# One core of a diffusion step: the RWKV scan with K and B transposed in the chain of states, row-half decay products, an unrolled tile loop and filler matmuls

## The chip, the cores and the metric

One Trainium2 chip, of which the program uses one core. The metric is the device time of one execution in microseconds (us); lower is better. TensorE is called PE, with its weight loads as PEld; VectorE is DVE, ScalarE is ACT, GpSimd is POOL, SyncE is SP.

## What is computed

One trunk layer for 512 latent tokens (`x_sample`) and 128 context tokens (`x_prompt`) with shared weights, all f32. The mixer projects the modulated input and feeds a Fourier branch and a bidirectional RWKV-7 scan with 16 heads of 64; both are merged, projected and normalised, and a mixture of 16 experts follows. The change is in the scan alone:

```python
def wkv7_scan(r, w, k, v, kk, a, s0, reverse):
    def step(S, inp):
        r_t, w_t, k_t, v_t, kk_t, a_t = inp
        sa = jnp.einsum('bhij,bhj->bhi', S, -kk_t)
        S = (S * w_t[:, :, None, :] + sa[..., None] * (kk_t * a_t)[:, :, None, :]
             + v_t[..., None] * k_t[:, :, None, :])
        y = jnp.einsum('bhij,bhj->bhi', S, r_t)
        return S, y
...
    w_log = -jax.nn.softplus(-(w_decay0 + jnp.einsum('btdr,drc->btdc', jnp.tanh(w_dn), w_decay_up))) - 0.5
    decay = jnp.exp(-jnp.exp(w_log))
    a_rate = jax.nn.sigmoid(a0 + jnp.einsum('btdr,drc->btdc', a_dn, a_up))
```

There is one scan per direction with its own decay and rate (`d` = 2 directions, rank `r` = 64 each).

## The kernel before

Four phases run one after the other: `front_phase` (projections, to about 445 us), `scan_phase` (to about 1400 us), `merge_phase`, and `expert_phase` with `combine_phase`. Only `scan_phase` (from L434) is touched.

**Tiling.** The 1024 channels are eight tiles of 128 (two heads each); the 640 tokens are five chunks of 128 (four latent, one context, `CT`). A scan over a chunk is written as matrix products. For each chunk, direction and head (four problems a chunk), masked pair products of K and B with R and the normalised key are made, a triangular 128x128 matrix is inverted by doubling, and then a short serial chain carries the state from chunk to chunk.

**One tile** is `body` on each engine:
- *Pair products* (`pair_products`, L874 to L889), chunk by chunk. DVE masks them (L1161), ACT copies the parts of the triangular matrix (L767, L768), and the output of the tile before is normalised between them (`norm`).
- *Six rounds of the inverse* (`z_step`, L905 and L911; `t_step`, L926 to L936) on three groups of chunks `b` = 0, 1, 2 (two, two and one chunk). POOL masks the block of each level (`m_off`, L668), and at the start makes the diagonal (`tt_start`, L649, L651) and the first T (`t_start`, L656, L660). ACT evicts Z (L776), DVE adds to the diagonal and to T (L1204, L1207, L1210).
- *The chain of states* (`part`): for the context, then latent chunks 0 to 3, X = products with V and the state (L952, L955), U = inverse times X (L961), S = the state's increment (L967: four 64x64 quadrant results), each for both directions. ACT copies X and U (L758, L761), DVE updates and scales the states (L1178, L1180, L1165, L1166). `output` (L976, L977, L981) is put between the steps. ACT evicts the output (L795) and the final states (L798).

**Front work of the next tile.** In the rounds of tile i, slots (three a round, one per group) hold the jobs that prepare tile i + 1. PE's job writes the PSUM tile `F[3]` (two banks, 1024 columns), ACT or DVE reads it and counts `s_free` up, and the next job waits for that; so jobs go strictly one by one, in the same order on PE, ACT and DVE. The slots are: decay of direction 0, norm of the keys, decay of direction 1, rates of both directions, V's transposes, the initial states', K's and B's transposes for direction 0, two empty for PE, K and B for direction 1, and the bonus. A decay or rate job is two matmuls on 64 of the 128 rows, of 512 and 128 columns (L821); a transposing job is five 128x128 transposes (L837). DVE does in the same slots the prefix sums (`decays`, L1062), `keys` (L1074 to L1082) and `operands` (L1089 to L1094). In each slot DVE does the front work first, and then waits for the products of the group.

**The loop.** Tiles 0 and 7 are written out; tiles 1 to 6 are a hardware loop with two tiles a turn on every engine (`tiles`, `Fori`), on SP another one. Semaphore targets inside it are computed from the loop's register.

```python
                for rd in range(TOP):
                    z_step(i, NGR * rd)
                    z_step(i, NGR * rd + 1)
                    for b in range(NGR):
                        if b == 1:
                            z_step(i, NGR * rd + 2)
                        if not last and PER_ROUND * rd + b < NSLOT:
                            front(PER_ROUND * rd + b, i + 1, 1 - m)
                        t_step(i, NGR * rd + b)
```

## Time and profile before

| | |
|---|---|
| time, median of 3 runs | 2767.99 us (2761.09 to 2768.16) |
| profiled execution | 2766.63 us, span 2764.8 us |
| mean granted clock of PE over the span | 0.927 |
| busy: PE / DVE / ACT / POOL | 2482.6 / 1002.9 / 612.9 / 358.5 us |
| instructions | 59730 |

The span runs from the first to the last instruction in the profile; some 1.8 us of the time lie around it. The granted clock is the share of TensorE's 2.4 GHz that the chip's throttle let through: 1.00 is 2.4 GHz and 0.50 is 1.2 GHz. Matmul durations are from start to a modelled end and overlap when matmuls follow each other, so a stretch is best priced from the start of one group to the start of the next. An f32 matmul is two instructions, a transpose is one. "issue" is idle time in which the engine waited for nothing that the profile shows.

### The profile page before, as it was taken

How to read it: one execution, taken by the hardware profiler on the slowest of the kernel's cores; microseconds unless marked ns; L12 is line 12 of the kernel's file. 1: busy time of each engine (PE TensorE's matmuls, PEld its weight loads, DVE VectorE, ACT ScalarE, POOL GpSimd, SP SyncE). 2: the span in 40 equal slices, each digit the busy share in tenths (PEclk: the TensorE clock that was granted, in tenths of full speed). 3: DMA queues.
4: the chain of work that ended last, by engine and by line, in shares of the span. 5: the costliest groups of instructions: out<-in, count | busy, mean ns of one | idle time of the engine just before them, and what ended most of it. 6: DMA issues, size and time to landing. Idle time of an engine off the chain costs nothing. (4 is left out here: it accounts for less than half of the span.)

```text
span 2764.8 us, 59730 instructions
## 1 busy us (share of the span) xinstructions
PE 2482.6 (90%) x26260; PEld 1565.3 (57%) x26260; DVE 1002.9 (36%) x1737; ACT 612.9 (22%) x1147; POOL 358.5 (13%) x405
## 2 busy tenths in 40 slices
PE   5999996888988888888959958999999999999993
PEld 3999985677777777877835432333333333333331
DVE  2344211747556475574411451111111222122114
ACT  2122222434435344353210010111111111111111
POOL 0000000414314043141200330000000000000000
PEclk8999997889889898898879969999999999999997
DMA  8363321000000000000073039999999999999984
GB/s 329 116 228 98 125 90 55 20 18 11 18 24 6 26 12 18 24 5 9 7 287 103 38 113 420 400 392 398 385 396 387 400 389 402 395 394 387 397 315 157
DMA packets 180734, 538.77 MB, mean 195 GB/s; under 512 B 13254, under 2 KB 53926, under 8 KB 180216
## 3 DMA queue, kind: packets, MB, share of 16 engines
q1 hardware_dynamic: 177400, 524.39, 49.1%
q0 software_dynamic: 3072, 10.49, 1.7%
q8 instruction: 213, 3.49, 0.5%
q14 instruction: 49, 0.40, 0.1%
HBM read 504.15 MB, written 30.70 MB: 193 GB/s over the span
## 5 line engine op out<-in xcount | busy, mean ns | idle before, releaser
L1699 PE MATMUL ps_h_lat<-w_piece,xT 128*64 128x512 f32 x2048 | 455.6, 598 | 8.9 <-DVE hidden L1821 7.5
L1699 PEld LDWEIGHTS ps_h_lat<-w_piece,xT 128*64 128x64 f32 x2048 | 145.6, 138 | 312.3 <-issue 312.3
L1724 PE MATMUL ps_y_lat<-w_piece,hiddenT 128*64 128x512 f32 x1024 | 232.6, 596 | 0.9 <-ACT hiddenT L1585 0.9
L1708 PE MATMUL ps_h_ctx<-w_piece,xT 128*16 128x512 f32 x2048 | 226.1, 593 | 0.0
L1815 DVE TENSOR_TENSOR hidden<-sigmoid_lat,ps_h_lat 64x1024 f32<-64x1024 f32 x32 | 39.1, 1223 | 506.8 <-ACT sigmoid_ctx L1591 506.8
L325 PE MATMUL ps_in<-hT_hi,w_in_hi 128*128 128x320 f32 x752 | 173.6, 312 | 3.0 <-issue 3.0
L668 POOL TENSOR_TENSOR Mo<-x,levels_sb 128x256 f32<-128x256 f32 x200 | 156.2, 803 | 129.8 <-PE ps_scan L905 129.8
L325 PE MATMUL ps_in<-hT_lo,w_in_hi 128*128 128x320 f32 x752 | 171.9, 310 | 0.0
L325 PE MATMUL ps_in<-hT_hi,w_in_lo 128*128 128x320 f32 x752 | 171.8, 310 | 0.0
L1724 PEld LDWEIGHTS ps_y_lat<-w_piece,hiddenT 128*64 128x64 f32 x1024 | 70.2, 137 | 138.3 <-issue 137.7
L930 PE MATMUL ps_scan<-Z,T 64*64 64x64 f32 x3200 | 127.0, 230 | 20.5 <-POOL T L660 12.7
L1708 PEld LDWEIGHTS ps_h_ctx<-w_piece,xT 128*16 128x16 f32 x2048 | 59.1, 97 | 139.7 <-issue 137.5
L905 PE MATMUL ps_scan<-TT_diag,Mo 64*64 64x64 f32 x3200 | 113.1, 222 | 27.8 <-issue 18.3
L1589 ACT ACTIVATE sigmoid_lat<-ps_h_lat 64x1024 f32<-64x1024 f32 x32 | 32.6, 1018 | 469.2 <-PE ps_h_lat L1699 469.2
L930 PEld LDWEIGHTS ps_scan<-Z,T 64*64 64x64 f32 x3200 | 111.6, 143 | 34.1 <-issue 29.9
L325 PEld LDWEIGHTS ps_in<-hT_hi,w_in_hi 128*128 128x128 f32 x752 | 126.1, 189 | 5.3 <-issue 5.1
L325 PEld LDWEIGHTS ps_in<-hT_lo,w_in_hi 128*128 128x128 f32 x752 | 126.4, 189 | 0.0
L325 PEld LDWEIGHTS ps_in<-hT_hi,w_in_lo 128*128 128x128 f32 x752 | 126.3, 189 | 0.0
L936 PE MATMUL ps_scan<-T,Z 64*64 64x64 f32 x3200 | 125.4, 230 | 0.0
L905 PEld LDWEIGHTS ps_scan<-TT_diag,Mo 64*64 64x64 f32 x3200 | 105.4, 139 | 30.4 <-issue 30.3
L1640 POOL DMA_INDIRECT x_scratch<-ye,row_out x16 | 22.8, 1428 | 737.5 <-DVE ye L1828 737.5
L1733 PE MATMUL ps_y_ctx<-w_piece,hiddenT 128*16 128x256 f32 x2048 | 116.7, 380 | 0.0
(276 smaller groups left out, 3605.6 us busy)
## 6 DMA issues: line engine op xcount, KB each, us to landing
w_piece<-in_w_e SPq DMA_DIRECT2D x192, 2048.0 KB, 14.0
w_ada<-in_w_ada SPq DMA_DIRECT2D x6, 4096.0 KB, 18.0
w_in_raw<-in_w_in SPq DMA_DIRECT2D x23, 1024.0 KB, 6.3
rkv_scratch<-projected SPq DMA_DIRECT2D x24, 320.0 KB, 6.4
rkv_T<-rkv_scratch SPq DMA_DIRECT2D x8, 960.0 KB, 5.1
gates_scratch<-projected SPq DMA_DIRECT2D x16, 320.0 KB, 6.8
gate_sb<-gates_scratch SPq DMA_DIRECT2D x8, 640.0 KB, 6.2
x<-in_x_sample SPq DMA_DIRECT2D x8, 512.0 KB, 5.7
```

The costliest lines, as they stand in the source:

```text
L325: last = pe.matmul(wide[c % 2][:, b * 512:b * 512 + HALF], w, h[:, k, b * HALF:(b + 1) * HALF], start=(k == 0 and n == 0), stop=(k == KD - ...
L668: ins = g_.tensor_tensor(Mo[:, p, :, :].rearrange("p (e h) n -> p e h n", e=2), Mq[:, ORDER[p], 0:2, :, :], levels[:, l, :, :].unsqueeze(2 ...
L905: last = pe.matmul(ps_of(b_z(b), b)[hs, c, q, :], Mo[hs, p, q, :], TD[hs, p, q, :], start=True, stop=True)
L930: last = pe.matmul(ps_of(b_z(b), b)[hs, c, q, :], T[hs, p, q, :], Z[hs, p, q, :], start=True, stop=True)
L936: last = pe.matmul(ps_of(b_dt(b), b)[hs, c, q, :], Z[hs, p, q, :], T[hs, p, q, :], start=True, stop=True)
L1589: act.activation(sg[UP, :], psA[UP, :], ACT.Sigmoid)
L1640: g_.indirect_dma_start(out=d["x1"], out_offset=bass.IndirectOffsetOnAxis(ap=row[j][:, 0:1], axis=0), in_=ye[j][:, :], in_offset=None, com ...
L1699: last = pe.matmul(psA[rows, cs], x[:, k, A], w[:, q, cs], start=(k == 0), stop=(k == KD - 1))
L1708: last = pe.matmul(psB[GRP[g], :], x[:, k, B], w[:, q, c * 512:(c + 1) * 512], start=(k == 0), stop=(k == KD - 1))
L1724: last = pe.matmul(psY[rows, :], hT[:, f, A], w[:, q, c * 512:(c + 1) * 512], start=(hf == 0 and f == 0), stop=(hf == 1 and f == FK - 1))
L1733: last = pe.matmul(psYB[GRP[g], 0:256], hT[:, f, B], w[:, q, g * 256:(g + 1) * 256], start=(hf == 0 and f == 0), stop=(hf == 1 and f == FK ...
L1815: v.tensor_tensor(hid[A, :], sg[UP, :], psA[UP, :], ALU.mult)
```

## The change

1. The loops are written out: all eight tiles on all engines, and SP's loop.
2. A decay or rate job does both directions at once. Direction 0 is on rows 0 to 63 and writes bank 0 of `F[3]`, direction 1 is on rows 64 to 127 and writes bank 1. The first job of each kind does 512 columns, the second 128. ACT evicts each with two activations. DVE's `decays` wait for both decay jobs, its `keys` for both rate jobs.
3. The transposes of K and B leave the slots. K of direction 0 is turned in the last round, B of direction 0 and K and B of direction 1 in the chain, between U and S of steps 0, 1 and 2. Before the first tile they stand behind the bonus.
4. S is two full 128x128 products for each direction instead of quadrant products (the parts across heads are not read).
5. `fill(n)`: n matmuls of 384 bf16 columns whose result nobody reads, into columns 640 to 1023 of `F[0]`, in the last round and in the chain. In the last tile they take the place of the transposes in the chain.
6. POOL starts T (`t_start`) directly behind each group's first mask instead of behind the masks of all groups.

```diff
-    (J_DEC0, J_NORM, J_DEC1, J_RATE0, J_RATE1, J_VT, J_ST, J_KT0, J_BT0, J_NONE0, J_NONE1, J_KT1, J_BT1, J_BONUS) = range(14)
+    (J_DEC0, J_DEC1, J_NORM, J_RATE0, J_RATE1, J_VT, J_ST, J_SCAN1, J_SUB1, J_KEYS1, J_NONE0, J_NONE1, J_NONE2, J_BONUS) = range(14)
+    TURNS = (J_KT0, J_BT0, J_KT1, J_BT1) = range(NSLOT, NSLOT + 4)
+    TURN_AT = {0: J_BT0, 1: J_KT1, 2: J_BT1}
@@ tiles (every engine; SP's loop in the same way)
-            body(0, 0, True, False)
-            with eng.Fori(0, (KD - 2) // 2) as j:
-                body(2 * j + 1, 1, False, False)
-                body(2 * j + 2, 0, False, False)
-            body(KD - 1, 1, False, True)
+            for i in range(KD):
+                body(i, i % 2, i == 0, i == KD - 1)
@@ POOL, body
                     m_off(b)
-                for b in range(NGR):
                     t_start(b)
@@ ACT, front
-                    act.activation(dst[:, :], ps, ACT.Sigmoid, bias=c[:, col:col + 1]).then_inc(s_free, 1)
+                    for dr in range(2):
+                        ins = act.activation(dst[dr][:, c0:c1], F[3][:, dr * 512:dr * 512 + c1 - c0], ACT.Sigmoid, bias=c[:, col + dr:col + dr + 1])
+                    ins.then_inc(s_free, 1)
-                for at, dr, which in ((J_RATE1, 0, (0, 1)), (J_VT, 0, (2,)), (J_BT0, 1, (0, 1)), (J_NONE1, 1, (2,))):
+                for at, dr, which in ((J_VT, 0, (0, 1)), (J_ST, 0, (2,)), (J_KEYS1, 1, (0, 1)), (J_NONE1, 1, (2,))):
@@ ACT, body
+                if not last:
+                    front(J_KT0, i + 1, 1 - m)
                 for n in CHAIN:
                     part(i, n, "X")
                     part(i, n, "U")
+                    if not last and n in TURN_AT:
+                        front(TURN_AT[n], i + 1, 1 - m)
@@ PE, front
-                    for c0, c1 in wide:
-                        last = pe.matmul(F[3][:, c0:c1], w[a:a + LORA, :], x[a:a + LORA, c0:c1], start=True, stop=True)
+                    for dr, rows in enumerate(HALVES):
+                        last = pe.matmul(F[3][:, dr * 512:dr * 512 + c1 - c0], w[rows, :], x[rows, c0:c1], start=True, stop=True)
@@ PE
+            def fill(n):
+                for _ in range(n):
+                    pe.matmul(F[0][:, TOK:1024], causal[:, 0, 0, :], causal[:, 0, :, :], start=True, stop=True)
+            def turn(n, i, m, last):
+                if not last:
+                    front(n, i + 1, 1 - m)
+                elif n != J_KT0:
+                    fill(3)
@@ PE, part, "S"
-                        for w, x in ((Bt[m][dr], U(dr, c)), (Kt[m][dr], Vt[m][:, c, :])):
-                            for hs in HALVES:
-                                last = pe.matmul(Sps[hs, hs], w[:, c, hs], x[:, hs], start=(w is Bt[m][dr]), stop=(w is Kt[m][dr]))
-                        last.then_inc(s_sn, 1)
+                        pe.matmul(Sps, Bt[m][dr][:, c, :], U(dr, c), start=True, stop=False)
+                        pe.matmul(Sps, Kt[m][dr][:, c, :], Vt[m][:, c, :], start=False, stop=True).then_inc(s_sn, 1)
@@ PE, body
                     z_step(i, NGR * rd + 1)
+                    if rd == TOP - 1:
+                        turn(J_KT0, i, m, last)
...
+                        if rd == TOP - 1 and b:
+                            fill(2)
                         t_step(i, NGR * rd + b)
+                fill(3)
                 pe.wait_ge(s_full, i * NGR + NGR)
                 part(i, m, CT, "X")
                 part(i, m, 0, "X")
+                fill(2)
                 part(i, m, CT, "U")
                 part(i, m, 0, "U")
+                turn(TURN_AT[0], i, m, last)
                 part(i, m, CT, "S")
                 part(i, m, 0, "S")
                 output(m, CT)
+                fill(1)
+                for n in (1, 2):
+                    part(i, m, n, "X")
+                    fill(2)
+                    part(i, m, n, "U")
+                    turn(TURN_AT[n], i, m, last)
+                    part(i, m, n, "S")
+                    if n == 1:
+                        fill(3)
                 output(m, 1)
+                fill(2)
                 part(i, m, 3, "X")
@@ DVE, front: the same work in other slots
+                if n == J_DEC1:
                     decays(i, 0, 0)
                 if n == J_NORM:
                     decays(i, 0, 1)
-                if n == J_DEC1:
+                if n == J_RATE0:
...
-                if n == J_RATE0:
+                if n == J_RATE1:
                     keys(i, m, 0)
-                if n == J_RATE1:
+                if n == J_VT:
                     operands(i, m, 0, (0, 1))
-                if n == J_VT:
+                if n == J_ST:
                     operands(i, m, 0, (2,))
-                if n == J_ST:
+                if n == J_SCAN1:
                     decays(i, 1, 0)
-                if n == J_KT0:
+                if n == J_SUB1:
                     decays(i, 1, 1)
-                if n == J_BT0:
+                if n == J_KEYS1:
                     keys(i, m, 1)
```

## Rows read from the trace of the kernel before

**Rows 1.** The page, busy tenths in 40 slices: TensorE's granted clock.

```profile
PEclk8999997889889898898879969999999999999997
```

**Rows 2.** The tile of the output, its eviction; duration min/median/max, first and last start.

```profile
L795 ACT ACTIVATE y_T<-ps_scan x8: 703/703/704, 608.3 to 1386.1; 128x640 f32<-128x640 f32 x8
```

**Rows 3.** Windows: length, busy us (instructions) by engine, granted clock, DMA share, GB/s.

```profile
857.12:872.15 15.03, 12.90 (x252) 10.84 (x254) 12.28 (x18) 9.40 (x11) 13.00 (x17) 0.89 0.01 2
893.03:905.93 12.90, 9.67 (x251) 9.10 (x249) 12.60 (x18) 4.24 (x9) 4.70 (x5) 0.87 0.01 3
905.93:914.90 8.97, 8.97 (x245) 8.07 (x243) 5.34 (x9) 2.28 (x4) 0.00 (x0) 1.00 0.01 4
919.84:952.38 32.54, 30.08 (x258) 27.20 (x258) 7.43 (x28) 5.55 (x21) 0.00 (x0) 0.74 0.11 34
1310.38:1355.46 45.08, 39.94 (x1280) 39.37 (x1280) 23.64 (x40) 10.98 (x24) 21.89 (x32) 0.96 0.03 11
```

**Rows 4.** Timeline, a middle tile's first round: start, duration, engine, operation, [idle before, releaser].

```profile
861.20 1.26 POOL L660 TENSOR_TENSOR T<-T,eye_sb 128x512 f32<-128x512 f32 x1
862.61 1.98 PE L930 MATMUL ps_scan<-Z,T 64*64 64x64 f32 x32 [2.13 <-POOL T L660]
867.89 1.15 PE L930 MATMUL ps_scan<-Z,T 64*64 64x64 f32 x32
869.90 1.34 PE L821 MATMUL ps_scan<-lora,w_dec 64*128 64x512 f32 x4
871.17 0.68 PE L930 MATMUL ps_scan<-Z,T 64*64 64x64 f32 x16
```

**Rows 5.** Timeline, PE, the last pair products of the same tile.

```profile
853.50 0.71 PE L874 MATMUL ps_scan<-AR,K 64*128 64x256 f32 x4
855.11 0.39 PE L883 MATMUL ps_scan<-B,AR 64*64 64x64 f32 x10
```

**Rows 6.** Timeline, DVE and PE, rounds one to four of the same tile.

```profile
862.73 4.40 DVE L1062 TENSOR_TENSOR_SCAN G_T<-one_sb,sg 128x128 f32<-128x128 f32 x5 [2.26 <-ACTq L698]
887.62 2.25 DVE L1062 TENSOR_TENSOR_SCAN G_T<-one_sb,sg 128x128 f32<-128x128 f32 x5
904.25 0.77 PE L837 MATMUL ps_scan<-ident_sb,K 128*128 128x128 f32 x5 [1.06 <-DVEq L1097]
906.63 0.41 DVE L1210 TENSOR_TENSOR T<-T,ps_scan 128x256 f32<-128x256 f32 x1
```

**Rows 7.** Timeline, PE: a front-phase product, and the chain at full clock.

```profile
439.81 0.46 PE L325 MATMUL ps_in<-hT_hi,w_in_lo 128*128 128x320 f32 x2
934.50 0.34 PE L967 MATMUL ps_scan<-x,Bt 128*64 128x64 f32 x4
944.63 0.44 PE L955 MATMUL ps_scan<-x,AR 128*128 128x128 f32 x2
944.90 0.56 PE L952 MATMUL ps_scan<-Vt,NRR 128*128 128x64 f32 x4
```

**Rows 8.** Timeline and windows: first pair products behind a jump, and without one.

```profile
838.36 0.95 PE L874 MATMUL ps_scan<-AR,K 64*128 64x256 f32 x4 [2.04 <-issue]
953.38 0.71 PE L874 MATMUL ps_scan<-AR,K 64*128 64x256 f32 x4 [1.00 <-ACT state_out L798]
838.36:842.62 4.26, 4.08 (x57) 3.53 (x57) 2.04 (x4) 0.00 (x0) 0.00 (x0) 0.60 0.12 21
953.38:955.77 2.39, 2.39 (x57) 2.20 (x57) 1.47 (x4) 0.00 (x0) 0.00 (x0) 1.00 0.08 14
```

**Rows 9.** Timeline, PE, before the first tile: B1's transposes, then the bonus.

```profile
494.15 1.33 PE L837 MATMUL ps_scan<-ident_sb,B 128*128 128x128 f32 x5 [0.79 <-ACT Kt L717]
496.27 2.50 PE L841 MATMUL ps_scan<-bonus,headones_sb 128*128 128x512 f32 x4 [0.79 <-ACT Bt L717]
```

**Rows 10.** Windows in the front phase, around 20 transposes of x.

```profile
50.40:53.50 3.10, 3.02 (x12) 1.85 (x10) 3.10 (x6) 2.51 (x6) 0.00 (x0) 0.50 1.02 410
53.50:56.00 2.50, 0.00 (x0) 0.00 (x0) 2.50 (x5) 2.42 (x6) 0.00 (x0) 0.97 1.02 410
```

More of the change, by code:

```diff
@@ L457, in scan_phase @@
     PER_ROUND = 3
-    (J_DEC0, J_NORM, J_DEC1, J_RATE0, J_RATE1, J_VT, J_ST, J_KT0, J_BT0, J_NONE0, J_NONE1, J_KT1, J_BT1, J_BONUS) = range(14)
+    (J_DEC0, J_DEC1, J_NORM, J_RATE0, J_RATE1, J_VT, J_ST, J_SCAN1, J_SUB1, J_KEYS1, J_NONE0, J_NONE1, J_NONE2, J_BONUS) = range(14)
     NSLOT = J_BONUS + 1
+    TURNS = (J_KT0, J_BT0, J_KT1, J_BT1) = range(NSLOT, NSLOT + 4)
     N_BONUS, N_GATE = 5, 6
-    JOBS = [n for n in range(NSLOT) if n not in (J_NONE0, J_NONE1)]
+    JOBS = [n for n in range(NSLOT + 4) if n not in (J_SCAN1, J_SUB1, J_KEYS1, J_NONE0, J_NONE1, J_NONE2)]
     NJ = len(JOBS)
@@ L610, in _ @@
             load_rkv(2)
-            with sp.Fori(1, KD - 2) as i:
+            for i in range(1, KD - 2):
                 store_states(i - 1)
@@ L691, in front @@
                 if n in (J_DEC0, J_DEC1, J_RATE0, J_RATE1):
-                    dst, col = {J_DEC0: (sg[0], C_DEC0), J_DEC1: (sg[1], C_DEC0 + 1), J_RATE0: (rate[0], C_RATE0),
-                                J_RATE1: (rate[1], C_RATE0 + 1)}[n]
+                    dst, col = (sg, C_DEC0) if n in (J_DEC0, J_DEC1) else (rate, C_RATE0)
+                    c0, c1 = wide[n in (J_DEC1, J_RATE1)]
                     done(n)
@@ L798, in body @@
                 act.activation(state_out[:, :, :], bank(5)[:, 0:2 * P].rearrange("p (e n) -> p e n", e=2), ACT.Copy).then_inc(s_sos, 1)
-            for n in range(NSLOT):
+            for n in range(NSLOT + len(TURNS)):
                 front(n, 0, 0)
@@ L817, in front @@
                     w, x = (w_dec, lora[0]) if n in (J_DEC0, J_DEC1) else (w_rate, lora[1])
-                    a = LORA * (n in (J_DEC1, J_RATE1))
+                    c0, c1 = wide[n in (J_DEC1, J_RATE1)]
                     pe.wait_ge(s_wup, 32 * i + 32)
-                    for c0, c1 in wide:
-                        last = pe.matmul(F[3][:, c0:c1], w[a:a + LORA, :], x[a:a + LORA, c0:c1], start=True, stop=True)
+                    for dr, rows in enumerate(HALVES):
+                        last = pe.matmul(F[3][:, dr * 512:dr * 512 + c1 - c0], w[rows, :], x[rows, c0:c1], start=True, stop=True)
                 if n == J_NORM:
@@ L1012, in body @@
                 output(m, CT)
-                part(i, m, 1, "X")
-                part(i, m, 1, "U")
-                part(i, m, 1, "S")
-                part(i, m, 2, "X")
-                part(i, m, 2, "U")
-                part(i, m, 2, "S")
+                fill(1)
[7 more added lines that the diff above has]
+                        fill(3)
                 output(m, 1)
+                fill(2)
                 part(i, m, 3, "X")
@@ L1031, in _ @@
             pe.wait_ge(s_masks, 1)
-            for n in range(NSLOT):
+            for n in range(NSLOT + len(TURNS)):
                 front(n, 0, 0)
@@ L1057, in decays @@
                 if half_ == 0:
-                    v.wait_ge(s_sig, 4 * i + (1, 2)[dr])
+                    v.wait_ge(s_sig, 4 * i + 2)
                     if dr == 1:
@@ L1071, in keys @@
             def keys(i, m, dr):
-                v.wait_ge(s_sig, 4 * i + 3 + dr)
+                v.wait_ge(s_sig, 4 * i + 4)
                 v.tensor_scalar(B[dr][:, :], rate[dr][:, :], -1.0, cur[m][:, C_KA:C_KA + 1], ALU.add, ALU.mult)
@@ L1130, in front @@
                 if n == J_BONUS:
-                    v.wait_ge(s_job, NJ * i + NJ)
+                    v.wait_ge(s_job, NJ * i + JOBS.index(J_BONUS) + 1)
                     v.tensor_tensor(bonus[m][:, :], ps[:, 0:TOK], v_, ALU.mult).then_inc(s_free, 1)
```

## The prediction

> **What bounds the kernel now.** The page comes first. The granted clock of TensorE (PEclk) is 9 or 10 tenths nearly everywhere, but reads 7 to 9 through slices 8 to 20, where the scan runs [rows 1]. The scan works through eight channel tiles in a row, and each evicts its output once. From the first eviction to the last there are (1386.1 - 608.3) / 7 = 111 us a tile [rows 2]. The change touches nothing outside this phase.
>
> Next the windows, cut at the borders of one middle tile and of the last one [rows 3]. Three things are to be seen. In the first round of triangular inverses (857.12 to 872.15) PE is busy for 12.9 of 15.0 us; in the fourth (893.03 to 905.93) for 9.7 of 12.9, while DVE is busy for 12.6. The last tile has no front work of a next tile, and does all six rounds in 45.1 us, against 919.84 - 857.12 = 62.7. And the chain of states (919.84 to 952.38) takes 32.5 us, of which PE is busy for 30.1, at a mean granted clock of 0.74. With two levels, 0.5 and 1.0, that is (1 - 0.74) x 2 x 32.5 = 16.9 us at 1.2 GHz. So TensorE is the bound of the chain, half of it at half clock, and DVE is the bound in the middle of the rounds.
>
> **The change part by part**, for a middle tile, first the rounds.
>
> *Start of T (POOL).* The first product with T waits 2.13 us for POOL, and then runs at half clock: 1.98 us for 32 matmul instructions, against 1.15 a little later [rows 4]; with the equal stretch behind it that is 2 x 0.83 = 1.7. The start of T now comes behind each group's first mask, some 7 us earlier for group 0. POOL then reaches the mask of group 2 later by two starts of T, of which the addition alone is 1.26 us [rows 4]; a PE job and the first T product stand before its user, so that costs nothing. Without that cover, in the last tile, I charge 1.5 us.
>
> *Decay and rate products.* One job of 640 columns takes 871.17 - 869.90 = 1.27 us [rows 4], so four are 5.1. On row halves the nearest row is the pair products, whose row halves also alternate: 4 x 384 columns in 855.11 - 853.50 = 1.61 us, 1.05 ns a column against 2.0 [rows 5]. The two directions together are 1280 columns: 1.34 us if they overlap as well as that, 2.54 if not at all. A single pair of long products overlaps only in its middle, so I take 1.75, which saves 0.8 for each kind, 1.6 a tile. ACT pays for it: four evictions become eight shorter ones. DVE's scan now waits for both decay jobs, so it starts about 2.3 us later than at 862.73 [rows 6]; but DVE has by then done the first two additions of the round.
>
> *K and B leave the rounds.* A transposing job is 0.77 us of PE, and that of K1 also waits 1.06 us for DVE's drain [rows 6]. Three leave the rounds outright; K0's stays in the last round, where PE waits for evictions anyway.
>
> *What DVE makes of it.* PE alone would gain 2.1 + 1.7 + 1.6 + 3 x 0.77 + 1.06 = 8.8 us. But DVE works almost without a pause from the scan at 862.73 to the last addition of round four at 906.63 + 0.41 [rows 6], and its work is only put in another order. I followed it slot by slot with the old durations: scan at 865.0, one scan at 4.40 us and one at 2.25 (the slow one runs beside POOL), and the last diagonal addition of round four at about 905.2. PE then has left one product of the third group (0.6, from its half size), the bonus job (1.3, like a decay job), the T products of the second group (869.90 - 867.89 = 2.0 [rows 4]) and of the third (1.1): 5.0 us, so it ends at 910.2, against 914.90 now [rows 3]. That is 4.7 us. PE now has gaps of some 2 us in rounds four and five where it waits for DVE; a fall of the clock there takes back up to 1.5. I take **4.0** a tile, with 1 and 8 as ends.
>
> **The chain.** Scaled to full clock, today's is 32.5 - 16.9 / 2 = 24.1 us. Added are:
> - S as full products: four instructions of 0.135 (two of this shape take 944.90 - 944.63 = 0.27) in place of eight that take about 0.32 (four of them are in sight for 0.34, tail included, and both halves overlap), so +0.22, eight times: 1.8 us [rows 7].
> - Three transposing jobs: 3 x 0.77 = 2.3 us.
> - 15 idle-filling products of 384 bf16 columns. No row shows one. The nearest is the one-instruction product of 320 columns in the front phase, two of which end within 0.46 us, at most 0.23 each and less where they overlap [rows 7]; the other bound is f32 at the decay job's 2.0 ns a column, 0.77. I take 0.18, near the first: 2.7 us. Seven more stand in the last round, in time in which PE waits.
>
> The sum is 30.9. About 1 us of the added work falls into waits that are in today's 32.5, but the step over DVE (state, scaled state, next X) keeps its length: I take **30.5**, a gain of 2.0. ACT's copies of K and B go behind the copies of U, while PE does S and output. The full gain hangs on the clock: h us at half clock cost h / 2.
>
> **The unrolled loop.** At its jump back PE stands for 2.04 us instead of 1.00, and the first pair products then run at half clock, 4.26 us instead of 2.39 [rows 8]. That is 2.9 us, at two places (the loop runs three times): 5.6 with rounding.
>
> **Prologue.** Tile 0's transposes of K0 and B0 lay beside DVE's work; now all four stand behind the bonus job and ahead of the first pair products. A job and its eviction are 496.27 - 494.15 = 2.12 us at half clock [rows 9]. Two more on the path are 4.2; the shorter row-half jobs give back about 1. I charge 3.
>
> **Sum.** Seven tiles with front work: 7 x (4.0 + 2.0) = 42. Jumps 5.6. Last tile: no decay job stands before its first T product, so the wait is 2.1 + 1.3, and 1.7 of half clock; less the 1.5 charged that is 3.6; its chain (fills in place of transposes) I leave as it is. Prologue -3. In all 48.2 us. The profiled execution took 2766.6 us (span 2764.8 and 1.8 around it), so **2718 us**. It lies 1.4 us below the median of the runs, 2767.99, which changes nothing.
>
> **The rivals.**
>
> *The clock stays up and DVE is not the bound (faster).* Rounds gain 6 to 7 rather than 4, because POOL's earlier end also frees DVE, and chains come to 29. That gives 48.2 + 7 x (2.5 + 1.5) = 76, 2690 us. For it: the last tile's rounds are 17.6 us shorter, so much of a middle tile's round is not its own work. Against: DVE's 12.6 of 12.9 us. Chance 0.2.
>
> *The clock falls once in each chain.* One stretch like today's second (8 us) costs 4 us a chain, 32 in all: 2750 us. For it: today the clock falls in waits and in the small X and U products, and these remain. Against: every such place now has a fill or wide columns beside it. Chance 0.2.
>
> *Half clock as often as today (slower).* If the added products don't keep the clock up, the chain has its 16.9 us at half clock and all the added work: 30.5 + 8.5 = 39.0, 6.5 longer than now, or 52 for eight chains. The gains outside the chains are 28 + 5.6 + 3.6 - 3 = 34, so the kernel ends 18 us slower: 2785 us. It decides from 4.2 us a chain, that is from some 12.5 us at half clock. For it: the chain is at half clock already with PE busy for nine tenths of it. Against it is the front phase: transposes alone, 12 of them between 50.40 and 53.50 at granted 0.50, and the clock then stands at 0.97 without anything else having run on PE [rows 10]. Chance 0.08. The Trainium skill ("TensorE: Matmul & The Clock Gate", Part 4: PE-mode transpose) states that transpose mode does not count as PE activity in the way that matmuls do. By that, the transposes in the chain would weaken it, and this rival would be the result; the row of the front phase speaks the other way.
>
> *The change doesn't do what it says:* the row halves run one behind the other (2.54 us for each kind). Then PE gains nothing there, but DVE's wait for both decays grows by 0.8: 7 x 0.8 = 6 us less gain, 2724. That lies inside the forecast.
>
> **How the numbers follow.** The forecast, 2718, has 0.5, with an own range of 2703 to 2737 (rounds' gain 2 to 6 us). The rivals have 0.2 (2690), 0.2 (2750), 0.08 (2785); 0.02 is left for the unforeseen. The range reaches to the inner parts of both large rivals: 2684 to 2752. Faster by over 0.3% (8.3 us, about what a measurement of this kernel can tell from no change) are all but the slower rival and the upper end of the clock rival: 0.87. Within 0.3%: 0.06, slower: 0.07.
>
> **What would show it.** Right: a period of 105 to 107 us from one eviction of the output to the next; windows over the chain at clock above 0.9 and 30 to 31 us long; no wait on POOL's T; pair products in 2.39 us at every tile's start; five transposes in the shadow of the U copies; PE waiting on DVE's additions in rounds four and five. Wrong: a chain of over 34 us, or a clock near 0.74 in it; DVE waiting longer for the sigmoids in round one than rounds four and five give back; fills of over 0.3 us each.

## The result, and the profile after

| | before | after |
|---|---|---|
| time, median of 4 runs | 2765.05 us (2761.09 to 2768.16) | 2687.45 us (2682.59 to 2688.05) |
| profiled execution | 2766.63 us, span 2764.8 | 2687.13 us, span 2685.2 |
| mean granted clock over the span | 0.927 | 0.961 |
| busy: PE / DVE / ACT / POOL | 2482.6 / 1002.9 / 612.9 / 358.5 us | 2420.9 / 984.9 / 615.4 / 363.8 us |

The medians are 77.6 us apart; the ratio estimated from all runs is 0.9706 [0.9686, 0.9727]. The direction was right. The time lies inside the outer range of 2684 to 2752 us, near its lower end, and outside the forecast's own 2703 to 2737; the gain is 1.6 times the 48 us worked out.

The page of the kernel after, its line of the granted clock and that of the output's eviction (the tile's view):

```profile
PEclk8999998799999999999889969999999999999997
```

```profile
L798 ACT ACTIVATE y_T<-ps_scan x8: 703/703/703, 601.4 to 1307.2; 128x640 f32<-128x640 f32 x8
```

The dip through the scan [rows 1] is gone: slices 9 to 19 (537 to 1275 us) all have a 9, the highest digit. From the first eviction to the last there are (1307.2 - 601.4) / 7 = 100.8 us a tile against 111 [rows 2].

Windows over tile 2 of the kernel after: its six rounds one by one, all six, the chain, and the first pair products of the tile; columns as in [rows 3]:

```profile
721.44:733.04 11.60, 10.53 (x253) 8.68 (x254) 8.40 (x14) 7.44 (x12) 10.12 (x15) 1.00 0.01 3
733.04:743.16 10.12, 9.91 (x260) 8.55 (x257) 9.61 (x15) 7.39 (x12) 5.09 (x5) 1.00 0.01 3
743.16:751.63 8.47, 7.74 (x248) 7.38 (x246) 7.80 (x13) 4.99 (x11) 4.81 (x5) 1.00 0.02 5
751.63:761.05 9.42, 7.84 (x248) 7.38 (x243) 9.05 (x17) 3.02 (x7) 4.37 (x5) 1.00 0.02 3
761.05:771.40 10.35, 8.60 (x228) 7.63 (x230) 10.01 (x16) 2.20 (x4) 0.00 (x0) 1.00 0.01 3
771.40:777.15 5.75, 5.61 (x116) 3.98 (x111) 2.93 (x6) 3.13 (x10) 0.00 (x0) 1.00 0.29 88
...
721.44:777.15 55.71, 50.24 (x1324) 43.60 (x1324) 47.79 (x76) 28.17 (x54) 24.40 (x30) 1.00 0.04 12
777.15:805.98 28.83, 27.28 (x253) 24.28 (x253) 7.42 (x28) 8.22 (x25) 0.00 (x0) 1.00 0.12 36
...
704.73:707.12 2.39, 2.39 (x57) 2.20 (x57) 1.46 (x4) 0.00 (x0) 0.00 (x0) 1.00 0.10 18
```

Against [rows 3]: the first round lost 15.03 - 11.60 = 3.4 us, the fourth 12.90 - 9.42 = 3.5. The fifth is longer, 10.35 against 8.97, and DVE is busy for 10.01 of it: the wait for DVE has moved there. The chain fell from 32.5 to 28.8 us, though three transposing jobs and 12 fills were added in it (three more fills stand ahead of it), and its clock is 1.00.

The same windows over all eight tiles, in us:

| stage | before | after | difference | foreseen |
|---|---|---|---|---|
| rounds, tiles 0 to 6 | 444.0 | 391.4 | -52.6 | -28 |
| rounds, last tile | 45.1 | 45.0 | 0 | -3.6 |
| eight chains | 252.3 | 230.4 | -21.9 | -14 |
| pair products and gaps ahead of them | 145.1 | 139.2 | -5.9 | -5.6 |
| start of the first pair products | 499.7 | 501.2 | +1.5 | +3 |

The mean of tiles 1 to 6 (called the middle tiles from here) is 63.4 us of rounds before and 55.9 after, and 31.9 and 28.8 of chain. So the miss is the rounds, and less of it the chains. The clock has a part in the rounds too: in the middle tiles it is 0.92 to 0.97 before and 1.00 after.

### The profile page after: what moved, and what is told of

Read it like the earlier page. It is cut to its first block and busy times, and to the rows that moved or that the text cites. A ratio compares the mean times of both kernels' runs of the same rounds, so it can differ in the third digit from the quotient of the medians.

```text
span 2685.2 us, 58051 instructions
## 1 busy us (share of the span) xinstructions
PE 2420.9 (90%) x26165; PEld 1504.4 (56%) x26165; DVE 984.9 (37%) x1737; ACT 615.4 (23%) x1179; POOL 363.8 (14%) x405
## 5 line engine op out<-in xcount | busy, mean ns | idle before, releaser
L666 POOL TENSOR_TENSOR Mo<-x,levels_sb 128x256 f32<-128x256 f32 x200 | 161.9, 832 | 99.2 <-PE ps_scan L908 99.1
L933 PE MATMUL ps_scan<-Z,T 64*64 64x64 f32 x3200 | 119.2, 221 | 5.9 <-ACT Z L775 5.3
L933 PEld LDWEIGHTS ps_scan<-Z,T 64*64 64x64 f32 x3200 | 106.1, 136 | 22.8 <-issue 19.5
L1186 DVE TENSOR_TENSOR NRR<-ps_scan,causal_sb 128x384 f32<-128x384 f32 x160 | 78.0, 548 | 106.2 <-PE ps_scan L878 106.0
L939 PE MATMUL ps_scan<-T,Z 64*64 64x64 f32 x3200 | 116.5, 219 | 0.4 <-issue 0.4
```

Source lines behind the costliest of these rows:

```text
L666: ins = g_.tensor_tensor(Mo[:, p, :, :].rearrange("p (e h) n -> p e h n", e=2), Mq[:, ORDER[p], 0:2, :, :], levels[:, l, :, :].unsqueeze(2 ...
L933: last = pe.matmul(ps_of(b_z(b), b)[hs, c, q, :], T[hs, p, q, :], Z[hs, p, q, :], start=True, stop=True)
L939: last = pe.matmul(ps_of(b_dt(b), b)[hs, c, q, :], Z[hs, p, q, :], T[hs, p, q, :], start=True, stop=True)
L1186: v.tensor_tensor(NRR[:, p, :, :], src[:, 0:3 * P].rearrange("p (a n) -> p a n", a=3), causal[:, dr, :, :], ALU.mult).then_inc(s_am, 1)
```

## The experiments

The measured values in one table; rounds and chain are means of the middle tiles. Before, after, the run without fills, before with fills, POOL's order and both prologue runs are medians of four runs; the others ran once. The kernel before alone ranged from 2757.7 to 2775.4 us over all its runs, so a single time says little, and the windows carry the argument.

| run | time | middle rounds | middle chain, clock |
|---|---|---|---|
| before | 2765.05 | 63.4 | 31.9, 0.74 to 0.78 |
| after | 2687.45 | 55.9 | 28.8, 1.00 |
| after, no fills | 2693.08 | 55.6 | 30.1, 0.84 to 1.00 |
| after, T late | 2701.96 | 58.2 | 28.8, 1.00 |
| before, with fills | 2742.71 | 63.4 | 28.5, 1.00 |
| after, transposes in slots, no fills | 2720.32 | 58.7 | 29.5, 0.79 to 1.00 |
| after, transposes in slots | 2704.51 | 58.8 | 28.6, 1.00 |
| after, one direction a job | 2700.47 | 57.0 | 28.8, 1.00 |
| after, POOL's order | 2687.48 | 55.8 | 28.8, 1.00 |
| after, loops | 2695.97 | 55.9 | 29.1, 1.00 |
| after, prologue | 2683.10 | 56.0 | 28.8, 1.00 |
| after, prologue, fewer fills | 2683.02 | 56.3 | 28.5, 1.00 |
| before, T early | 2757.20 | 61.1 | 31.6, 0.74 to 0.78 |
| before, unrolled | 2755.21 | 63.4 | 31.0, 0.73 to 0.83 |

Theory A is the prediction's: DVE bounds the middle of the rounds and hides most of what PE saves. Theory B is the rival that DVE is not the bound and the clock stays up.

### Without fills

```diff
-                for _ in range(n):
+                for _ in range(0):
```

> The changed kernel without its filler products (the transposes and the full products of S stay in the chain). Theory A, the fillers hold the clock: the chain's granted clock falls from 1.00 to under 0.9 and the chain (28.8 us) gets longer, 29 to 32 us, although it has 15 products of 0.16 us less; the kernel is 5 to 30 us slower than the changed one. Theory B, the wide products of S and the transposes hold it alone: clock 1.00, chain 26.5 to 27.5 us, the kernel 10 to 20 us faster than the changed one.

2693.08 us, ratio to before 0.9737 [0.9720, 0.9754]. Windows over the chains of tiles 1, 2 and 3:

```profile
674.85:702.75 27.90, 25.85 (x241) 23.16 (x241) 7.43 (x28) 8.24 (x25) 0.00 (x0) 1.00 0.12 38
...
775.70:808.13 32.43, 30.38 (x241) 27.66 (x241) 7.42 (x28) 8.25 (x25) 0.00 (x0) 0.84 0.10 33
...
881.56:912.40 30.84, 28.79 (x241) 26.04 (x241) 7.42 (x28) 8.25 (x25) 0.00 (x0) 0.89 0.11 35
```

The same 241 instructions take 27.90 us where the clock stays at 1.00 (three of the eight chains) and up to 32.43 where it falls. So the fills (12 of the 15; three stand ahead of the first X) cost 28.83 - 27.90 = 0.93 us a chain and 0.3 in the rounds, and save up to 4.5 where the clock would have fallen. Where it falls, the timeline of the second of these chains shows:

```profile
775.70 1.55 PE L967 MATMUL ps_scan<-Vt,NRR 128*128 128x64 f32 x12 [0.65 <-ACT x L787]
...
778.34 1.81 PE L976 MATMUL ps_scan<-Xs,x 128*128 128x64 f32 x8
780.68 1.97 PE L976 MATMUL ps_scan<-Xs,x 128*128 128x64 f32 x8 [0.53 <-ACT Xs L757]
```

U is 1.81 us at half clock against 1.00 at full, behind the waits for ACT at the chain's start. The fills are worth 2693.08 - 2687.45 = 5.6 us net here. Without them the loss is small because the work that the change brings into the chain already holds the clock in part: over tiles 0 to 6 the chains' mean clock is 0.93 here, against 0.75 in the kernel before.

### Start of T late again

```diff
                     m_off(b)
+                for b in range(NGR):
                     t_start(b)
```

> The changed kernel with T started behind the masks of all groups again. Theory C, POOL's place decides about DVE: the wait for T returns (about 2.1 us), the clock falls in round one, DVE's scans lengthen again (2.8 and 1.7 us to above 3.5 and 2.2), and the rounds of a middle tile go from 55.8 to 60 us or more. Theory D, only the wait itself: rounds 57 to 58 us, DVE's durations unchanged. The last tile's rounds (45.0) change by less than 1 us under both.

2701.96 us. The middle rounds grow by 2.3 us and DVE's busy time in them is the same, 47.7 against 47.8. PE in the first round of tile 2 of this kernel:

```profile
729.71 1.57 PE L934 MATMUL ps_scan<-Z,T 64*64 64x64 f32 x26 [2.45 <-issue]
```

The wait is back, at the place of [rows 4], with some half clock behind it. The DVE timeline shows how it reaches the end: every addition to the diagonal, from the first to the fifteenth, starts 2.4 to 3.3 us later after the start of the rounds than in the changed kernel. DVE's scan waits for the sigmoids, they wait for the decay jobs, and those for the T product. So DVE's chain of work does not hide a wait in round one; it is moved by it as a whole. Theory A had a DVE that goes on while PE waits. Part of the 2.3 us is clock: the two middle tiles at 1.00 take 57.5 us, 1.8 more than the changed kernel's 55.7, and the four at 0.94 or 0.97 take 58.4 to 58.7.

### The kernel before with fills

```diff
+            def fill(n):
+                for _ in range(n):
+                    pe.matmul(F[0][:, TOK:1024], causal[:, 0, 0, :], causal[:, 0, :, :], start=True, stop=True)
@@ body: in the last round and the chain, at the places of the change, three for each turn in the chain
```

> The kernel before with filler products at the places of the changed kernel (three more where that one has transposes). Theory A, the clock is the matter of the chain: granted clock near 1.00 in the chains, 27 to 29 us each instead of 30.3 to 32.7; rounds unchanged; 25 to 40 us faster than before. Rival: the clock still falls in the narrow X and U products, chain 33 to 36 us, 10 to 30 us slower than before.

2742.71 us, ratio 0.9916 [0.9897, 0.9936]. A window over the chain of tile 3 of this kernel:

```profile
911.00:939.63 28.63, 25.89 (x279) 21.69 (x279) 7.42 (x28) 5.56 (x21) 0.00 (x0) 1.00 0.13 38
```

Against the 32.54 us of [rows 3], 21 more instructions and 3.9 us less. The eight chains lose 252.3 - 227.2 = 25.1 us, which is the whole gain, and the rounds stay at 63.4. Fills alone give more in the chains than the change does (21.9), since S and the transposes aren't lengthened or added. They give a little under a third of its gain of 79.6 us in the span.

### Transposes back in the slots, without and with fills

```diff
-    (..., J_ST, J_SCAN1, J_SUB1, J_KEYS1, J_NONE0, J_NONE1, J_NONE2, J_BONUS) = range(14)
+    (..., J_ST, J_KT0, J_BT0, J_KEYS1, J_NONE0, J_NONE1, J_KT1, J_BT1, J_BONUS) = range(15)
-    TURN_AT = {0: J_BT0, 1: J_KT1, 2: J_BT1}
+    TURN_AT = {}
```

> The changed kernel without fillers and with the transposes of K and B back in slots of the rounds, one by one. If transposes count as activity for the clock, the chain has a lower granted clock here than in the run without fillers; if they do not count (the rule of the Trainium skill), it is equal or higher. With the clock as in the kernel before (0.74 to 0.78) the chain is 30 to 32 us, at full clock about 25. Rounds get longer by the four jobs: 57 to 60 us instead of 55.8.

> The changed kernel with the transposes of K and B back in slots of the rounds (three fillers stand in their places in the chain). From the pair of runs without fillers (58.7 against 55.6 us) the rounds of a middle tile are about 3.2 us longer than the changed kernel's 55.9, so 59; the chain is 28.4 us as in the kernel before with fillers, clock 1.00. If instead the moved jobs only filled PE's waits, the rounds stay under 57.

2720.32 us without fills and 2704.51 us with. Against their counterparts with the transposes in the chain the middle rounds grow by 3.2 and 2.9 us. At full clock the chain is 26.53 us without transposes and without fills (two of eight chains), against 27.90 with: 0.46 us for each transposing job. With fills in the transposes' place it is 28.62 against 28.83. So four jobs moved out of the slots save 2.9 us and cost 0.2 as long as something has to hold the clock anyway. Of the 2.9 us about 1 is clock: the rounds with fills and transposes in slots take 57.6 us where they are at 1.00 and up to 60.5 at 0.94.

The two runs without fills bear on the clock. Windows over the chains of tiles 1, 2 and 5, transposes in slots, no fills:

```profile
683.46:710.00 26.54, 24.62 (x226) 21.81 (x226) 7.43 (x28) 5.45 (x21) 0.00 (x0) 1.00 0.15 46
...
785.12:815.74 30.62, 28.98 (x226) 26.30 (x226) 7.43 (x28) 5.46 (x21) 0.00 (x0) 0.83 0.13 40
...
1102.93:1135.00 32.07, 30.43 (x226) 27.70 (x226) 7.43 (x28) 5.45 (x21) 0.00 (x0) 0.79 0.12 38
```

Over tiles 0 to 6 the mean clock of the chains is 0.87 here, and 0.93 with the three transposing jobs between U and S (the last tile has none in either kernel). The transposes did not weaken the clock; that they helped it is not shown by seven chains of each, of which two and three stood at 1.00. The Trainium skill ("TensorE: Matmul & The Clock Gate", Part 4: PE-mode transpose) states that a transpose does not count as PE activity in the way a matmul does, and by that the chains with transposes would stand lower. With [rows 10] this is the second place of this case that does not agree with it.

### One direction for each decay and rate job

```diff
-                    for dr, rows in enumerate(HALVES):
-                        last = pe.matmul(F[3][:, dr * 512:dr * 512 + c1 - c0], w[rows, :], x[rows, c0:c1], start=True, stop=True)
+                    a = LORA * (n in (J_DEC1, J_RATE1))
+                    for c0, c1 in wide:
+                        last = pe.matmul(F[3][:, c0:c1], w[a:a + LORA, :], x[a:a + LORA, c0:c1], start=True, stop=True)
```

> The changed kernel with one direction for each decay or rate job, 640 columns on 64 rows, in the new order of slots. If row halves save PE time on the path: rounds of a middle tile 1.0 to 2.5 us longer than 55.9. If DVE sets the rounds: under 0.5 us longer, since DVE waits for both jobs in any case and PE has gaps of 4 us in rounds three to five. The jobs themselves go from 1.05 + 0.42 to 1.27 + 1.27 us.

2700.47 us; the middle rounds grow by 1.1 us (56.7 to 57.0 us in the four tiles at 1.00, against 55.7 to 56.4). Tile 0's rounds grow by 5.5, at a clock of 0.92 against 1.00, and the first pair products start 2.2 us later. In the changed kernel PE's timeline has the two jobs of a kind:

```profile
723.46 1.13 PE L824 MATMUL ps_scan<-lora,w_dec 64*128 64x512 f32 x4
724.51 1.15 PE L933 MATMUL ps_scan<-Z,T 64*64 64x64 f32 x32
...
727.27 0.68 PE L908 MATMUL ps_scan<-TT_diag,Mo 64*64 64x64 f32 x16 [0.67 <-POOL Mo L666]
728.35 0.49 PE L824 MATMUL ps_scan<-lora,w_dec 64*128 64x128 f32 x4 [0.40 <-ACT sg L695]
728.77 0.33 PE L933 MATMUL ps_scan<-Z,T 64*64 64x64 f32 x4
```

Start to start they take 724.51 - 723.46 = 1.05 and 728.77 - 728.35 = 0.42 us, 1.47 a kind for 1280 columns: 1.15 ns a column. The row halves do overlap, nearly as well as the pair products.

### POOL's order

In the last tile PE waits at a new place, 6 us after the start of the rounds (timeline of the changed kernel):

```profile
1239.81 0.68 PE L908 MATMUL ps_scan<-TT_diag,Mo 64*64 64x64 f32 x15 [2.08 <-POOL Mo L666]
...
1240.39 1.81 PE L933 MATMUL ps_scan<-Z,T 64*64 64x64 f32 x30
```

That is group 2's mask, which POOL now makes behind two starts of T, and half clock behind the wait. The run puts the starts of groups 1 and 2 behind it:

```diff
                 for b in range(NGR):
                     m_off(b)
-                    t_start(b)
+                    if b == 0:
+                        t_start(0)
+                t_start(1)
+                t_start(2)
```

> The changed kernel with T of groups 1 and 2 started behind the mask of group 2. In the changed kernel the third product waits 0.67 us for that mask in middle tiles and 2.08 us in the last tile, where the clock then falls. Expected: those waits gone, rounds of a middle tile 0.5 to 1.1 us shorter, the last tile's 2 to 4 us; 6 to 10 us faster than the changed kernel. Against it: T of group 1 comes later than its user, and a wait of the same size appears at the T product of group 1: under 2 us.

2687.48 us, ratio 0.9710 [0.9683, 0.9737]: no difference. In the middle tiles the wait of 0.67 us for the mask is gone, but the second decay job then waits 0.74 for ACT instead of 0.40. In the last tile a wait of 1.31 us for T and one of 0.54 for the masks of round two replace the one of 2.08. POOL is simply behind PE there, in either order.

### The loops back

```diff
-            for i in range(KD):
-                body(i, i % 2, i == 0, i == KD - 1)
+            body(0, 0, True, False)
+            with eng.Fori(0, (KD - 2) // 2) as j:
+                body(2 * j + 1, 1, False, False)
+                body(2 * j + 2, 0, False, False)
+            body(KD - 1, 1, False, True)
```

> The changed kernel with the hardware loops put back. At the two jumps back PE stands for about 1 us more and the first pair products run at half clock (1.9 us): 5 to 6 us slower, in the pair stages of tiles 3 and 5 alone. If the chain's full clock carries over the jump, only the stand remains: 2 us.

2695.97 us; the last tile ends 8.1 us later. PE behind the second jump back (timeline):

```profile
1019.29 0.71 PE L880 MATMUL ps_scan<-AR,K 64*128 64x256 f32 x4 [2.43 <-issue]
1020.04 0.90 PE L880 MATMUL ps_scan<-AR,K 64*128 64x256 f32 x4
```

The stand is like that of [rows 8], and the pair products behind it run partly at half clock: the stage takes 18.8 us, against 16.7. Behind the first jump the stage takes 18.1 us at a clock of 1.00, so there it is not the clock; PE stands once more in it, for 0.72 us. The two jumps cost 6.1 us in all (2.6 in the gaps, 3.5 in the stages). The looped tiles without one also lose 0.3 us in the pair products, and all six 0.3 in the chain, where no jump is near. That makes 9.0 us; the start, tile 0 and the last tile's rounds (43.2 us against 45.0, the same instructions) differ besides.

### The kernel before with T early, and the kernel before unrolled

```diff
                     m_off(b)
-                for b in range(NGR):
                     t_start(b)
```

> The kernel before with the start of T put directly behind each group's first mask and nothing else changed. Undoing this part in the changed kernel cost 2.3 us a tile in the rounds. If the parts of the rounds' gain add up, the six middle tiles' rounds fall here from 63.4 to about 61.1 us and the span by 16 us, to 2749. If DVE takes it back in the middle of the rounds (the theory of the prediction: PE alone gains more than the rounds do), they fall by less than 1 us and the span by less than 8.

2757.20 us, span 2755.4. The middle rounds fall to 61.1 us: 2.3, as much as the undoing cost in the changed kernel. So this part is worth the same in both kernels. Here too some of it is clock (0.97 to 1.00 in the middle rounds, 0.92 to 0.97 before). The last tile ends 1385.9 - 1371.4 = 14.5 us earlier, near the 16 expected. The span falls only by 9.4: the other 5 us are lost behind the scan, in phases that the edit doesn't touch.

> The kernel before with its loops of tiles written out and nothing else changed. Putting the loops back into the changed kernel cost 8.5 us: about 5 at the jumps and 0.3 us for each chain and pair stage of a looped tile. I expect 8 us less here, a span of 2757, with the pair stages of tiles 3 and 5 at 17 us and the two long gaps ahead of them gone. If instructions that take their semaphore targets from a register also cost time in the rounds, these become shorter than 63.4 by up to 1.2 us, which is what the other parts leave unexplained of the rounds' gain, and the span falls by 15.

2755.21 us, span 2753.4. The edit is that of the loops, the other way round. The pair stages are 16.7 us in tiles 1 to 7, the long gaps are gone, and the rounds are 63.4 us as before: unrolling is no part of their gain. From the first pair products to the last tile's end it is 886.2 - 875.8 = 10.4 us less, of which 3.6 are the chains (248.7 against 252.3): up to 1.7 by the 0.3 us of each looped chain, the rest the clock's chance.

### Prologue, and fewer fills

The timeline of the changed kernel ahead of its first tile has four jobs in a row, each 2.1 us at half clock:

```profile
493.60 1.33 PE L840 MATMUL ps_scan<-ident_sb,K 128*128 128x128 f32 x5 [0.92 <-DVE bonus L1157]
495.73 1.33 PE L840 MATMUL ps_scan<-ident_sb,B 128*128 128x128 f32 x5 [0.79 <-ACT Kt L716]
497.85 1.33 PE L840 MATMUL ps_scan<-ident_sb,K 128*128 128x128 f32 x5 [0.79 <-ACT Bt L716]
499.97 1.33 PE L840 MATMUL ps_scan<-ident_sb,B 128*128 128x128 f32 x5 [0.79 <-ACT Kt L716]
501.23 1.23 PE L877 MATMUL ps_scan<-AR,K 64*128 64x256 f32 x4
```

```diff
+    FIRST = list(range(J_ST + 1)) + [J_KT0, J_BT0] + list(range(J_ST + 1, J_BONUS)) + [J_KT1, J_BT1, J_BONUS]
-            for n in range(NSLOT + len(TURNS)):
+            for n in FIRST:
```

> The changed kernel with one other order of the jobs of tile 0, before the first tile: the transposes of K0 and B0 follow those of the initial states, those of K1 and B1 stand ahead of the bonus job instead of behind it. Tiles 1 to 7 are as they were. The run with all transposes in the slots reached its first pair products at 496.9 us against 501.2, so I expect the first pair products at 497 to 498 and the time 3.5 to 4.5 us under that of the changed kernel: 2683 us. The rival: the prologue is bound by DVE and the pair products start at most 1 us earlier, 2687 us.

2683.10 us (2681.99 to 2684.76), ratio 0.9705 [0.9674, 0.9736]. The first pair products start at 497.2, 4.0 us earlier, but the last tile ends only 2.5 us earlier: the clock is 0.94 and 0.97 in the rounds of tiles 0 and 1, where it was 1.00. That is not shown to come of the new order: with the old one the clock in tile 0's rounds is also 0.94 in the runs with POOL's order and with loops, and their first pair products start at 502.1 and 501.7. The medians are 4.3 us apart, but the spreads of the two kernels overlap, and the estimated ratios to the kernel before are 0.9705 and 0.9706. That this version is faster as a whole is not shown.

```diff
                 output(m, CT)
-                fill(1)
...
                 output(m, 1)
-                fill(2)
```

> As the run before it, and three of the fifteen idle-filling products of a chain are left out: the one behind the output of the context and the two behind the output of chunk 1, where outputs of full width have just run. If those outputs hold the granted clock by themselves, the chain loses about 3 x 0.16 us less whatever lay in waits: 28.4 to 28.6 us against 28.8, clock 1.00 in all eight, and the time is 2 to 3 us under that of the run before. If the fills hold the clock there, some chains fall to 0.8 to 0.9 as without any fill and are 30 to 32 us long, and the time is 5 us or more over that of the run before.

2683.02 us, ratio 0.9704 [0.9672, 0.9735]. The chains are 28.50 us and at 1.00, so these three fills held nothing in them. But the 2.6 us won are not in the time: tiles 3 and 5 now also have a fall of the clock in their rounds (0.97), each some 0.7 us, and 1.6 us more lie behind the scan, which the edit doesn't touch.

## Why the prediction was right or wrong

**Start of T (right in kind, and DVE did not hide it).** The wait of 2.13 us and the half clock behind it are gone: the first T product follows the decay job without idle time. PE's own saving was worked out as 3.8; 2.3 arrived in the rounds, in both kernels alike. A new wait of 0.67 us for the mask of group 2, priced at nothing, stands in the first round; where the rest went is not shown.

**Decay and rate products (right).** 1.47 us a kind against 1.75 foreseen, and 1.1 us of rounds against the 1.6 of PE alone. That the row halves run one behind the other did not happen.

**K and B leave the rounds (right).** 2.9 us of rounds, about 1 of it clock, of the 3.4 that PE alone was given for them.

**"What DVE makes of it" (the step that failed).** It took 4.0 us of PE's 8.8; measured are 63.4 - 55.9 = 7.5. Three undone parts give 2.3 + 2.9 + 1.1 = 6.3, almost 2 of it by clock; the other 1.2 were not isolated (the order of the jobs and the pairing of evictions went with them). The term that was mis-sized is the time at which DVE reaches the last addition to the diagonal in round four. Followed slot by slot with old durations it came 48.1 us after the start of the rounds. In tile 2 it comes 45.2 after:

```profile
730.09 2.81 DVE L1086 TENSOR_TENSOR_SCAN G_T<-one_sb,sg 128x128 f32<-128x128 f32 x5 [2.75 <-ACTq L697]
...
751.01 1.68 DVE L1086 TENSOR_TENSOR_SCAN G_T<-one_sb,sg 128x128 f32<-128x128 f32 x5
...
766.63 0.41 DVE L1229 TENSOR_TENSOR TT_diag<-TT_diag,ps_scan 128x256 f32<-128x256 f32 x1
```

The last row is that addition: 766.63 - 721.44 = 45.2. The first scan starts 8.65 us after the start of the rounds, where 7.9 were foreseen, but the two take 4.49 us together and not 6.65 as in [rows 6]. DVE's busy time in the middle rounds fell from 50.3 to 47.8 us for the same instructions. With the later start of the scan, the last addition comes 48.1 - 45.2 = 2.9 us before the time worked out. The 0.7 charged for falls of the clock in PE's new gaps did not come, the clock is 1.00. And the base was low: tile 3 has 62.7 us of rounds, the mean 63.4, which holds more falls of the clock. These are 4.3 us for the missing 3.5; 0.8 is taken back in round six, which with K0's transposes and the fills is 5.75 us against 4.94. DVE was indeed nearly without a pause there, and PE does wait 1.04 and 1.52 us in the first products of rounds four and five (timeline of PE), each until 0.10 us after one of DVE's additions has ended:

```profile
753.80 1.15 PE L908 MATMUL ps_scan<-TT_diag,Mo 64*64 64x64 f32 x32 [1.04 <-issue]
...
763.71 0.41 PE L908 MATMUL ps_scan<-TT_diag,Mo 64*64 64x64 f32 x6 [1.52 <-issue]
```

So the bound was named rightly and its length taken as fixed, which it was not. What sets the length of the scans is POOL's work beside them. POOL's timeline around the first scan of the tile, before (the scan runs from 862.73 to 867.13) and after (from 730.09 to 732.90):

```profile
862.42 1.41 POOL L656 TENSOR_TENSOR T<-x,levels_sb 128x256 f32<-128x256 f32 x2
863.97 1.27 POOL L660 TENSOR_TENSOR T<-T,eye_sb 128x512 f32<-128x512 f32 x1
866.81 3.88 POOL L668 TENSOR_TENSOR Mo<-x,levels_sb 128x256 f32<-128x256 f32 x5
...
728.57 3.41 POOL L666 TENSOR_TENSOR Mo<-x,levels_sb 128x256 f32<-128x256 f32 x5
734.23 4.30 POOL L666 TENSOR_TENSOR Mo<-x,levels_sb 128x256 f32<-128x256 f32 x4 [2.24 <-PE ps_scan L908]
```

Before, POOL is busy during all five scans, the one beside its addition of 512 columns taking 1.48 us. After, it is done at 731.98: three scans take 0.70 to 0.82 us, the two behind them 0.39 each. It is so in the traces of all 14 kernels: a group of five with no POOL instruction beside it takes 1.68 or 1.69 us, whatever ACT does, and the others take 2.10 to 4.44. The edits that move POOL's instructions and nothing else move the first scan: 4.40 to 3.78 us with T early in the kernel before, 2.81 to 2.97 or 3.62 with T late and to 3.16 with POOL's other order in the changed one. Other work of DVE from SBUF behaves alike (the product `rate`, 0.82 alone and 1.29 beside POOL); the additions that read PSUM do not (0.68 either way). The prediction had noted that the slow scan runs beside POOL, moved POOL's starts of T ahead of it, and kept 4.40 and 2.25 us.

**The chain (clock right, size too small).** 28.8 us against 30.5. S costs 0.11 us an instruction rather than 0.135, as the timeline has it:

```profile
782.29 0.72 PE L840 MATMUL ps_scan<-ident_sb,B 128*128 128x128 f32 x5
782.84 0.39 PE L980 MATMUL ps_scan<-x,Bt 128*128 128x128 f32 x2
783.06 0.39 PE L981 MATMUL ps_scan<-Vt,Kt 128*128 128x128 f32 x2
783.29 0.39 PE L980 MATMUL ps_scan<-x,Bt 128*128 128x128 f32 x2
```

A direction is 783.29 - 782.84 = 0.45 us, and a transposing job 0.55 rather than 0.77. On the path the three jobs cost 1.4 us (2.3 foreseen) and the fills 0.9 (2.7). The rest of the sum was 24.1 + 1.8 = 25.9 and measured 26.5, without jobs and fills at full clock. The price of a fill itself was near, two take 0.33 us, 0.16 each against 0.18; but three of the 15 stand ahead of the chain (they were counted among the seven of the last round as well), and of the other twelve (1.9 us) half lie in waits. The last tile's chain, which I left as it was, gained too: its fills hold the clock, 28.6 against 30.8.

**The unrolled loop (right, too small).** 5.6 foreseen (its own terms, 2.9 twice, give 5.8); the two jumps cost 6.1, and the 0.3 us a stage that looped tiles lose besides, 2.9 in all, were not foreseen. On the last tile's end it was 8.1 us.

**The last tile (wrong).** Foreseen was a gain of 3.6 with 1.5 charged for POOL. POOL's mask of group 2 is 2.08 us late and has half clock behind it, as the T had, and POOL's other order gives 45.0 us too. The size is not sharp: the same instructions take 43.2 to 45.4 us in the six kernels that have them, T early alone brought 45.1 to 43.9 in the kernel before, and without the seven fills it is 43.7. So a part of the gain is there, and the fills may take it back.

**Prologue (right).** Four transposing jobs at 2.1 us stand behind the bonus. The +1.5 of the table is one pair of executions: with this prologue the first pair products start at 501.2 to 502.7 us in five kernels, with that of before at 496.9 to 500.7 in four, 2.9 on average, and 3 were foreseen. What the shorter jobs give back is lost in that spread.

**The rivals.** What came is the first one, "the clock stays up and DVE is not the bound", in its time (2690 foreseen) and its rounds (6 to 7 us) and chains (29), though its reason is only half right: DVE still bounds the middle, with shorter instructions. Its own "for", the last tile's rounds, was no evidence. That the clock falls once a chain is what happens without fills. Half clock in the chains as often as today did not come in any run that has fills.

## What to carry to other kernels

- A wait in the first stage of a pipelined stretch passes to its end even if a second engine is busy throughout the middle, when that engine's work starts behind the wait. Ask what its first instruction waits for before hiding a saving behind its busy share.
- Durations of the bounding engine are not constants. When a change moves what runs beside it, look up in the trace what stood beside the long and the short instances, and price the new places by that: here a scan beside POOL took up to 1.48 us and one alone 0.39.
- Where short dependent steps let the clock fall, fills at those waits are cheap (0.9 us a chain) against the fall (up to 4.5), and useful work that has to be done anyway is better than a fill: the transposes took its place for 0.2 us.

## What was not expected of the hardware

- The same five 128x128 scans on DVE take from 1.68 us, with POOL idle, to 4.44 with POOL busy throughout.
- An instruction stream in a loop costs 0.3 us more in a pair stage and in a chain than the same stream written out, at places with no jump near.
- Equal work does not get an equal clock: equal chains of 241 instructions stood at 1.00 or at 0.84 in one execution, and the rounds of tile 0, with the same work for PE, stood at 1.00 in the changed kernel and at 0.94 in the runs with loops, with POOL's order and with the new prologue.
